# A router's rows on other engines, its logits and first list in another form, and small wait changes in a two-layer decoder trunk

## The reference

```python
h = h + short_conv_mixer(rms_norm(h, norm_mix[0]), ...)          # layer 0
h = h + dilated_attention_mixer(rms_norm(h, norm_mix[1]), ...)   # layer 1
# after each of them:
t = rms_norm(h, norm_ffn[i])
coarse_prob = softmax(t @ w_coarse + b_coarse)
p_top, g_top = top_k(coarse_prob, 1)
fine_logits = (einsum("nd,gde->nge", t, w_fine) + b_fine)[g_top]
f_val, f_idx = top_k(fine_logits, 2)
gate = p_top * softmax(f_val)
h = h + sum over the two experts e of gate * ((silu(t @ w_gate[e]) * (t @ w_up[e])) @ w_down[e])
# at the end: rms_norm(h, norm_final)
```

## Time and profile before

| | |
|---|---|
| median of 3 runs | 1418.67 us (1417.36 to 1419.28) |
| the profiled execution | 1418.97 us, of which the span of the trace is 1417.0 |
| TensorE (PE) busy | 1356.8 us, 96% of the span |
| VectorE (DVE) | 1007.8 us, 71% |
| ScalarE (ACT) | 787.1 us, 56% |
| GpSimd (POOL) | 201.3 us, 14% |
| granted TensorE clock, mean | 0.977 of full speed |
| HBM read and written | 291.19 MB and 31.46 MB |

### The profile page before, as it was taken

One profiled execution on the slowest core, in us unless ns is written; L12 is line 12 of the kernel. 1 busy time (PEld: TensorE's weight loads), 2 busy tenths in 40 slices (PEclk: granted clock), 3 DMA queues, 4 the chain that ended last, 5 costly groups with the idle time before them and its releaser, 6 DMA issues.

```text
span 1417.0 us, 20605 instructions
## 1 busy us (share of the span) xinstructions
PE 1356.8 (96%) x7151; PEld 1120.4 (79%) x7151; DVE 1007.8 (71%) x1362; ACT 787.1 (56%) x977; POOL 201.3 (14%) x309
## 2 busy tenths in 40 slices
PE   7999988999999999999999999999998899999995
PEld 6888877888888877888888778888777688888883
DVE  6656478999999996252558535344866899999998
ACT  5222245888888843533357253324724488888882
POOL 3000021111111312020200111120002111111121
PEclk9999987999999999999999999999998799999998
DMA  5238427999999964232210222231025799999994
GB/s 209 89 119 309 183 84 261 352 388 391 393 391 389 380 240 158 73 107 89 90 60 2 90 89 90 89 115 65 2 75 208 275 370 385 395 387 387 390 345 178
DMA packets 85090, 307.88 MB, mean 217 GB/s; under 512 B 12146, under 2 KB 12170, under 8 KB 68645
## 3 DMA queue, kind: packets, MB, share of 16 engines
q1 hardware_dynamic: 75936, 291.19, 55.5%
q0 software_dynamic: 8640, 15.86, 2.9%
q10 hardware_dynamic: 452, 0.02, 0.0%
HBM read 291.19 MB, written 31.46 MB: 228 GB/s over the span
## 4 chain that ended last, share of the span: by engine, by line
PE 89%; DVE 5%; issue 3%; DMA 1%; ACT 1%; SPq 0%; DVEq 0%; POOLq 0%; POOL 0%; ACTq 0%
PE ps L326 27%; PE ps L328 26%; PE ps L327 26%; PE ps L1881 2%; PE ps L1662 2%; PE ps L1864 1%; DVE probT L1450 1%; PE ps L1956 1%; PE ps L1557 1%; PE ps L1846 1%; DVE h L1232 1%; DMA x_rows<-hn_rows,tok_col 1%; PE ps L1849 1%; PE ps L1677 1%; PE ps L1686 1%
## 5 line engine op out<-in xcount | busy, mean ns | idle before, releaser
L326 PE MATMUL ps<-W_hi,xT_hi_all 128*128 128x512 f32 x1408 | 560.2, 398 | 7.1 <-DVE xT_lo_all L1166 4.7
L328 PE MATMUL ps<-W_hi,xT_lo_all 128*128 128x512 f32 x1408 | 551.7, 392 | 0.0
L327 PE MATMUL ps<-W_lo,xT_hi_all 128*128 128x512 f32 x1408 | 550.1, 391 | 0.0
L1158 DVE TENSOR_TENSOR W_lo<-m_raw,W_hi 128x2048 fp32r<-128x2048 f32 x192 | 435.8, 2290 | 49.2 <-ACT W_hi L728 48.1
L728 ACT ACTIVATE W_hi<-m_raw 128x2048 fp32r<-128x2048 f32 x192 | 367.1, 1914 | 43.4 <-PE ps L328 43.0
L326 PEld LDWEIGHTS ps<-W_hi,xT_hi_all 128*128 128x128 f32 x1408 | 265.4, 188 | 67.5 <-issue 5.5
L328 PEld LDWEIGHTS ps<-W_hi,xT_lo_all 128*128 128x128 f32 x1408 | 265.5, 189 | 57.6
L327 PEld LDWEIGHTS ps<-W_lo,xT_hi_all 128*128 128x128 f32 x1408 | 265.8, 189 | 51.7
L683 ACT ACTIVATE W_hi<-raw,mix_gain 128x512 fp32r<-128x512 f32 x192 | 123.0, 712 | 290.8 <-issue 278.6
L957 DVE SCALAR_TENSOR_TENSOR W_lo<-raw,mix_gain,W_hi 128x512 fp32r<-128x512 f32 x192 | 132.5, 751 | 211.6 <-ACT W_hi L683 208.9
L649 POOL TENSOR_TENSOR qk_rot<-rope_a,rope_b 128x512 f32<-128x512 f32 x48 | 62.2, 1302 | 365.4 <-DVE rope_b L1518 365.4
(11 more groups left out here) (250 smaller groups left out, 1407.7 us busy)
## 6 DMA issues: line engine op xcount, KB each, us to landing
m_raw<-in_w_gate_dram SPq DMA_DIRECT2D x64, 1024.0 KB, 8.0
m_raw<-in_w_up_dram SPq DMA_DIRECT2D x64, 1024.0 KB, 8.9
m_raw<-in_w_down_dram SPq DMA_DIRECT2D x64, 1024.0 KB, 9.0
raw<-in_attn_w_qkv_dram SPq DMA_DIRECT2D x36, 1024.0 KB, 5.0
raw<-in_conv_w_in_dram SPq DMA_DIRECT2D x12, 1024.0 KB, 5.2
y_rows<-zero_rows SPq DMA_DIRECT2D x2, 4096.0 KB, 17.5
y_pick<-y_rows SPq DMA_DIRECT2D x16, 512.0 KB, 7.3
raw<-in_conv_w_out_dram SPq DMA_DIRECT2D x4, 1024.0 KB, 7.5
```

Of the source, the lines that this page charges most:

```text
L326: pe.matmul(o, a_hi, b_hi, start=first, stop=False)
L327: pe.matmul(o, a_hi, b_lo, start=False, stop=False)
L328: return pe.matmul(o, a_lo, b_hi, start=False, stop=last)
L1158: dve.tensor_tensor(MW_lo[c % MSPLIT][:, :, :], m_raw[c % MRAW][:, :, :], MW_hi[c % MSPLIT][:, :, :].bitcast(F), ALU.subtract).then_inc(s[ ...
```

## The change

Eight edits. (1) hn of row tiles 2 and 3 is made by GpSimd (h times gain, both read with a stride) and then ScalarE (times rstd, in place, dense); VectorE makes only tiles 0 and 1. GpSimd computes rstd of tile 2, that product, rstd of tile 3, and its product. SP stores tiles 2 and 3 when ScalarE is done. (2) In `route` logits 1 are copied before the lo part of row tile 3, and a copy `first_id` of `dest_id` in fp32r with two equal columns stands between them. (3) `first_oh` is fp32r, and the list matmuls have two columns. (4) The first expert's rows are turned, copied and subtracted in two halves, each with its own signal; the counts of the later rows go up by one. (5) ScalarE signals each of the first three pieces of a hi part that carries a gain, and VectorE's pieces wait for them one by one. (6) Half of the sixteen statistics copies go to ScalarE; two semaphores of that exchange are one. (7) `heads_hi` and `heads_lo` stand at u = 1, 9 and 2, 10, not 2, 6 and 4, 8. (8) The convolution's loop on TensorE is written out, and rstd is turned in its first chunk alone.

```diff
@@ -251,7 +251,8 @@
...
-        first_oh = at("first_oh", [P, NT, P], F, FG + 14 * KB)
+        first_oh = at("first_oh", [P, NT, P], FR, FG + 14 * KB)
+        first_id = temp("first_id", [P, NT, 2], FR)
@@ -468,9 +470,12 @@
...
-            def store_rows(first):
+            def store_rows(l):
                 for r in range(NT):
-                    sp.wait_ge(hn_ready, first + r + 1)
+                    if r < 2:
+                        sp.wait_ge(hn_ready, 2 * l + r + 1)
+                    else:
+                        sp.wait_ge(row_scaled, 2 * l + r - 1)
@@ -623,12 +628,12 @@
...
-                pool.wait_ge(s["turned"], 1)
+                pool.wait_ge(s["turned"], 2)
                 gather(1)
-                pool.wait_ge(s["turned"], 2)
+                pool.wait_ge(s["turned"], 3)
...
                 with pool.Fori(2, later) as i:
-                    pool.wait_ge(s["turned"], i + 1)
+                    pool.wait_ge(s["turned"], i + 2)
@@ -652,13 +657,16 @@
...
                 first = 8 * l + 4
-                rstd_tiles(first)
+                rstd_tile(first, 0)
+                rstd_tile(first, 1)
                 pool.wait_ge(gain_in, 16 * (k + 1))
-                pool.wait_ge(hn_ready, 4 * l + 3)
-                pool.wait_ge(row_scaled, l + 1)
-                row = hn[1][:, :].rearrange("p (k q) -> p k q", k=KD)
-                pool.tensor_tensor(row, row, gain[:, :].rearrange("p (q k) -> p k q", k=KD), ALU.mult
-                                   ).then_inc(hn_ready, 1)
+                for r in range(2, NT):
+                    rstd_tile(first, r)
+                    pool.wait_ge(hn_stored[r % 2], 32 * l + 16)
+                    pool.tensor_tensor(hn[r % 2][:, :].rearrange("p (k q) -> p k q", k=KD),
+                                       h[:, r, :].rearrange("p (q k) -> p k q", k=KD),
+                                       gain[:, :].rearrange("p (q k) -> p k q", k=KD), ALU.mult
+                                       ).then_inc(row_gained, 1)
@@ -682,6 +690,8 @@
...
                                              scale=norm_weight(uc, rev, k))
+                        if k < 3:
+                            ins.then_inc(hi_piece, 1)
@@ -710,11 +720,11 @@
...
                 turn_hi(stage, 3)
-                act.wait_ge(rstd_ready, first + 4)
-                act.wait_ge(hn_stored[1], 32 * l + 16)
-                act.activation(hn[1][:, :].rearrange("p (k q) -> p q k", k=KD),
-                               h[:, 3, :].rearrange("p (q k) -> p q k", k=KD), ACT.Copy, scale=rstd[:, 3:4]
-                               ).then_inc(row_scaled, 1)
+                for r in range(2, NT):
+                    act.wait_ge(row_gained, 2 * l + r - 1)
+                    act.wait_ge(rstd_ready, first + r + 1)
+                    act.activation(hn[r % 2][:, :], hn[r % 2][:, :], ACT.Copy, scale=rstd[:, r:r + 1]
+                                   ).then_inc(row_scaled, 1)
@@ -736,8 +746,12 @@
...
+                def first_rows_hi(a):
+                    act.wait_ge(s["turned"], a + 1)
+                    act.activation(xT_hi_all[:, FIRST_X + a, :], ps[:, 2 + a, :], ACT.Copy).then_inc(s["xhi"], 1)
+
                 def rows_hi(i, at=0):
-                    act.wait_ge(s["turned"], i + 1)
+                    act.wait_ge(s["turned"], i + 2)
@@ -762,7 +776,8 @@
...
-                rows_hi(0, FIRST_X)
+                first_rows_hi(0)
+                first_rows_hi(1)
@@ -884,11 +899,16 @@
...
                         softmax_exp(u + 1, s)
-                    if s == 1 and u in (2, 6):
-                        heads_hi(u // 4)
+                    if s == 1 and u in (1, 9):
+                        heads_hi(u // 8)
+                for t in range(2):
+                    for r in range(NT):
+                        ins = act.activation(stat[32 * t:32 * t + 32, 0, r, :, :],
+                                             near_stat[32 * r:32 * r + 32, t, :, :], ACT.Copy)
+                ins.then_inc(stat_copied, 1)
                 hi(U_QKV + 7, s * 3 + 2)
-                act.wait_ge(gap_in, s + 1)
-                act.activation(stat_exp[:, :, :, :], stat_exp[:, :, :, :], ACT.Exp).then_inc(gap_out, 1)
+                act.wait_ge(gap_step, 2 * s + 1)
+                act.activation(stat_exp[:, :, :, :], stat_exp[:, :, :, :], ACT.Exp).then_inc(gap_step, 1)
@@ -949,11 +969,19 @@
...
+            pieces_read = [0]
+
             def lo(uc, rev=0):
-                dve.wait_ge(split_hi, rev * 6 + uc + 1)
+                if not normed(uc, rev):
+                    dve.wait_ge(split_hi, rev * 6 + uc + 1)
...
                     for k in range(4):
+                        if k < 3:
+                            pieces_read[0] += 1
+                            dve.wait_ge(hi_piece, pieces_read[0])
+                        else:
+                            dve.wait_ge(split_hi, rev * 6 + uc + 1)
@@ -988,19 +1016,13 @@
...
                 turn_lo(stage, 2)
-                norm_row(k, first, 2)
...
                 if r >= 2:
-                    if first < 16:
-                        dve.wait_ge(x_turned, first + r - 1)
-                    if first in (4, 12):
-                        dve.wait_ge(hn_stored[r % 2], (32 if first == 12 else 0) + 16)
-                    if first == 16:
-                        dve.wait_ge(out_stored[r % 2], 16)
+                    dve.wait_ge(out_stored[r % 2], 16)
@@ -1044,8 +1066,9 @@
...
                 logits_copy(l, 0)
+                logits_copy(l, 1)
+                dve.tensor_copy(first_id[:, :, :], bc(dest_id[:, 0], 2))
                 turn_lo(stage, 3)
-                logits_copy(l, 1)
@@ -1161,8 +1184,13 @@
...
+                def first_rows_lo(a):
+                    dve.wait_ge(s["xhi"], a + 1)
+                    dve.tensor_tensor(xT_lo_all[:, FIRST_X + a, :], ps[:, 2 + a, :],
+                                      xT_hi_all[:, FIRST_X + a, :].bitcast(F), ALU.subtract).then_inc(s["xlo"], 1)
+
                 def rows_lo(i, at=0):
-                    dve.wait_ge(s["xhi"], i + 1)
+                    dve.wait_ge(s["xhi"], i + 2)
@@ -1452,15 +1481,16 @@
...
                 dve.wait_ge(expd, s * 64 + 64)
-                for t in range(NT):
+                for t in range(2, NT):
...
                 after(last)
+                dve.wait_ge(stat_copied, s + 1)
...
                 dve.tensor_tensor(stat_exp[:, :, :, :], stat_min[:, :, :].unsqueeze(1).to_broadcast([P, 2, NT, 8]),
-                                  stat[:, :, :, 0, :], ALU.subtract).then_inc(gap_in, 1)
-                dve.wait_ge(gap_out, s + 1)
+                                  stat[:, :, :, 0, :], ALU.subtract).then_inc(gap_step, 1)
+                dve.wait_ge(gap_step, 2 * s + 2)
@@ -1498,8 +1528,8 @@
...
                     probs_back(u, s)
-                    if s == 1 and u in (4, 8):
-                        heads_lo(u // 4 - 1)
+                    if s == 1 and u in (2, 10):
+                        heads_lo(u // 8)
@@ -1630,7 +1660,7 @@
...
                 for r in range(NT):
-                    ins = pe.matmul(ps[:, 4, 0:1], first_oh[:, r, :], dest_id[:, 0, r:r + 1], start=(r == 0),
+                    ins = pe.matmul(ps[:, 4, 0:2], first_oh[:, r, :], first_id[:, r, :], start=(r == 0),
@@ -1656,11 +1686,13 @@
...
-                def turn_x(i):
+                def turn_x(i, halves=False):
...
                                            x_rows_r[:, k * P:(k + 1) * P], ident_r[:, :])
+                        if halves and k == 3:
+                            ins.then_inc(s["turned"], 1)
@@ -1706,9 +1738,10 @@
...
-                turn_x(0)
-                pe.wait_ge(s["xlo"], 1)
+                turn_x(0, True)
                 for j in range(3):
+                    if j < 2:
+                        pe.wait_ge(s["xlo"], j + 1)
@@ -1765,7 +1798,7 @@
...
             pe.transpose(ps[:, 7, 0:24], conv_rows[:, :], ident[0:24, 0:24]).then_inc(conv_t, 1)
-            with pe.Fori(0, 2) as c:
+            for c in range(2):
@@ -1781,7 +1814,7 @@
...
                         ins.then_inc(unit_done, 1)
-                        if uc == 0:
+                        if uc + c == 0:
```

More of the change, by code:

```diff
@@ L299, in build @@
             sem("pv_done"), sem("o_stored"))
-        gap_in, gap_out, scales_ready, spread, merged = (
-            sem("gap_in"), sem("gap_out"), sem("scales_ready"), sem("spread"), sem("merged"))
+        gap_step, scales_ready, spread, merged = sem("gap_step"), sem("scales_ready"), sem("spread"), sem("merged")
         scales_turned, scales_copied = sem("scales_turned"), sem("scales_copied")
+        stat_copied = sem("stat_copied")
         logits_copied, logits_turned = sem("logits_copied"), sem("logits_turned")
-        row_scaled = sem("row_scaled")
+        row_scaled, row_gained = sem("row_scaled"), sem("row_gained")
+        hi_piece = sem("hi_piece")
         mix_gain_in, ident_ready, rstd_turned = sem("mix_gain_in"), sem("ident_ready"), sem("rstd_turned")
```

(4 more changed lines are left out.)

7 lines of the change are left out of this document (3 added, 4 removed).

## The result

| | before | changed |
|---|---|---|
| median | 1418.81 us (1417.36 to 1419.28, 4 runs) | 1409.79 us (1408.63 to 1410.33, 4 runs) |
| ratio | | 0.9939, 95% interval 0.9925 to 0.9953 |
| span of the profiled execution | 1417.0 us | 1408.2 us |
| mean granted clock | 0.977 | 0.982 |

The change is faster by 9.0 us, where 13.2 were forecast. 1409.8 lies in the range of 1402.8 to 1413.0, but outside the forecast's own 1403 to 1408.5.

A forecast was written before the change was run, and what follows sets the result against it. TensorE is busy for 96% of the span, so only its idle or wasted stretches, chiefly the two routers, can be won. 1418.97 - 8.9 (routers) - 4.3 (rest) = 1405.8 us; own range 1403 to 1408.5, whole range 1402.8 to 1413.0.

The forecast's parts named there:

- the last logits, up to the ranking: Each router: with row 2 off VectorE and logits reordered, the last logits begin at 202.4, not 203.68; 1.25 us.
- the ranking's first step: Each router: VectorE's subtraction, held until GpSimd's product ends, falls from 1.94 to 0.5 us; 1.45 us won.
- first list, tok_col: Each router: four fp32r passes replace eight, but VectorE is not free sooner than 0.5 us before tok_col; 0.5 us.
- gather: Each router: the earlier gather may meet SP's two weight loads, costing 0 to 1.3 us; 0.2 taken.
- first rows in halves: Each router: first product of expert 0 comes 2.2 us after the rows land, not 3.65; 1.45 us.
- x: Length of one GpSimd product for tiles 2 and 3 in the router; 3.2 us taken, between 2.86 and 4.2.
- Rival 2: Routers: products of 4.2 us hold the ranking's first step, 1.65 us later in each; 1409.1 us, chance 0.10.
- Rival 1: Routers: GpSimd's tile 3 product holds the copy first_id if x is under 2.95; 1412.1 us, chance 0.27.
- Rows 7: Profile rows cited: a copy from SBUF took 1.15 us beside GpSimd's memset (0.95) and 0.23 alone.
- The rotary rows: TensorE's wait of 1.5 us for them goes, since VectorE's lo part follows ScalarE's pieces; 1.6 us with its restart.
- The rstd matmuls: Convolution: eight matmuls that turn rstd run once instead of twice; 0.8 us.
- The clock: After each router: its rise may shift up to 2 us against the first product; 0, plus or minus 1 each.

The follow-up runs named there:

- loads_after_gather: The changed kernel with SyncE's wait for the first gathered rows ahead of the first weight load behind the stored rows, instead of the third: 1407.93 us.
- scales_as_before: The changed kernel with all sixteen statistics copies on VectorE again: 1411.38 us, ratio 0.9952 to the kernel before.

## Why the prediction came out as it did

**What was right.** Every part of the change acts where the prediction put it, and the sign was right. The measured gathers of the first router vary by 0.8 us from kernel to kernel, so that its -0.63 is uncertain by as much; the -1.34 of the second repeats. From row 3 of h to the first product, by steps, first and second router:

| step | forecast | measured |
|---|---|---|
| the last logits, up to the ranking | 1.25 | 1.02, 1.23 |
| the ranking's first step | 1.45 | 0.38, 0.15 |
| first list, tok_col | 0.5 | 0.48, 0.48 |
| gather | -0.2 | -0.63, -1.34 |
| first rows in halves | 1.45 | 1.47, 1.47 |
| router | 4.45 | 2.72, 1.99 |

**The term that was mis-sized is x**, GpSimd's product with two strided inputs. Forecast 3.2, "a second such step" on top of the 2.86 with one; it takes 4.07 and 3.84. Two dense operands cost 2.4, as the prediction had it (2.5), but the second stride costs 1.1, the first 0.45. What came (3.84 over 2.36 is 1.63, 4.07 over 2.41 is 1.69) is near the factor of 1.7 that stood as the upper bound. That is chance: the bound was taken from VectorE's product of 2.06 us, which by the code (`norm_row`) reads both inputs in straight order and writes with a stride, while GpSimd's reads both with a stride and writes in straight order. No row of before had a product of that kind. So it was Rival 2 in its mechanism: the second product's end is 205.41, or 206.1 on the scale of before, where its formula 198.1 + 2x has 206.0. It was given 0.10, too little. The rule in the Trainium skill (GPSIMD Engine Reference, Performance pitfalls for Q7 kernels), 50% more for wide steps, gave an estimate of 3.75 and was nearer than my 3.2; measured with two such operands it is 63 to 69% more. That the time came within 0.7 us of Rival 2's 1409.1 is in part luck: the hold cost 2.4 of the 3.3 us that it had there, and the gathers, the rotary rows and the logits lost 2.9 more, of which the clock and the small terms gave back 1.2. Nor did the second router repeat the first within 0.2 us in each step: its first ranking step took 1.71 before, so only 1.2 could be won there, and its gather 4.95.

**The gather's term** was the second. "I take 0.2, since the queues have room" was wrong: 0.63 and 1.34 of the up to 1.3 came, and the queues were full (422 GB/s in the second router's stretch). The prediction saw that tile 3's store would come nearly 2 us earlier and take the loads with it. The dear product took this away too: on the scale of before the loads start at 208.1 instead of 208.3, while the gather is issued 1.9 us earlier. These two terms are one chain, and loads_after_gather removes the second half of it, clearly in the second router.

**Rival 1 was not what limited the changed kernel, but its mechanism is real.** At x near 4 the copy is done before the second product starts, as the prediction's arithmetic has it (free above 2.95). The two kernels that made x small or early show it held for 2.03 and 2.99 us. The rule of the Trainium skill (SBUF — State Buffer, Who interferes with whom) agrees with these rows, and with the 0.32 of the changed kernel, where the copy ends with the first product. Rows 7, which the prediction called in for the order, show the hold alone: the copy's record there begins 0.12 us ahead of the memset's. What the prediction did not draw from it: its own forecast had only 0.35 us of room between "x over 2.95" for the copy and "x up to 3.3" for the ranking. With x = 2.4 the copy is held, with x = 4 the ranking. A forecast that needs a price without a row to lie between 2.95 and 3.3 should have had less than 0.60.

**The rotary rows**: forecast 1.6, measured 0.5. The step that failed is "What is late next is nothing". VectorE was to be free at 538.0; taken to the changed kernel's time, which is 4.1 us earlier there, that is 533.9, and it was free at 535.06. It stood in the wait for gain_p, whose load came 1.2 us later against the rows around it than before. That is no chance: in all ten kernels that load it at this place VectorE stands idle for 2.50 to 2.62 us there. Why the load takes 3.6 us from its issue, where it took 2.4 before, is open. The idle stretch was in the trace of before too, where it lasted 1.15, and ended well ahead of the old limit: a wait that costs nothing is a candidate for what is late next.

**The rest.** The rstd matmuls are gone from the convolution's second pass. At row 3 of h the profiled execution is 0.70 ahead, but the start-up hides part of it. From the rstd matmuls of the first chunk (29.98 before, 30.20 in the changed kernel) to row 3 of h it was 168.01 us and is 167.09, and between 167.04 and 167.10 in all thirteen kernels that have this part: 0.92 for the forecast's 0.8. Scales 1.3 by the wait for 1.4; heads 0.8 for 0.5. The clock, put at 0, gave 0.68 in experts 1 and 0.20 in experts 2, since it rose 3.3 and 4.2 us behind the first product instead of 6.1 and 5.1. Across all kernels here that distance is between 2.9 and 6.1, with no order in it that I could find; why is open. Its price is less than the forecast's half: by straight lines through the fourteen kernels a rise that comes 1 us later makes the first experts' stage 0.28 us longer and the second 0.37.

**The sum.** Of 13.2 us, 2.4 went at the ranking's first step, 1.6 at the gathers, 1.1 at the rotary rows, 0.25 at the logits; 0.9 came from the clock, 0.3 from the heads and 0.1 from the convolution, and 0.1 was lost at the scales. That leaves 9.05, and the medians differ by 9.0.

## What to carry to other kernels

When work is moved to GpSimd to free VectorE, price its stride for each operand, and then list every VectorE operation that lies beside it and reads and writes SBUF alone: here, making the GpSimd operation faster or earlier moved the hold to another of them, until the small copy on the critical path went to ScalarE. A step that comes earlier meets what used to be over or not yet begun: here a wait ahead of the next loads was worth 1.6 us at the second gather, more than the 1.1 that the freed ranking brought there. And look for idle stretches that end shortly before the limit you remove.

## What the runs showed of the hardware that was not expected

- GpSimd's product of 128x1024 float32: 2.36 to 2.41 us dense, 2.85 with one strided input, 3.83 to 4.10 with both inputs strided (a step of 32 bytes).
- The hold goes both ways: beside a VectorE product of 2.08 us a GpSimd operation on one column took 1.78 us (0.19 alone), and a VectorE copy of eight columns took 2.99 beside a GpSimd product, 0.15 alone.
- An indirect gather of 128 rows of 4 KB is there 4.2 to 4.6 us after its issue with the loads over or not yet begun, and up to 6.7 (scales_as_before) when two loads of 1 MB were issued 4.4 us before it.
